# Score matmuls of a sparse-attention layer, all on 128 rows

## The reference, cut to what matters

```
s_c = jnp.einsum('bghqd,bgnd->bghqn', qblk, k_c) * scale + head_bias(rel_c)
...
s_s = jnp.einsum('bghqd,bgqkd->bghqk', qblk, k_sel) * scale + bias_s
...
s_w = jnp.einsum('bghqd,bgkd->bghqk', qblk, k_wb) * scale + head_bias(rel_w)
...
return gblk[..., 0:1] * o_c + gblk[..., 1:2] * o_s + gblk[..., 2:3] * o_w
```

## Time and profile before

| | |
|---|---|
| median of 3 runs | 2231.28 us (2228.06 to 2240.76) |
| the profiled execution | 2240.75 us, its span 2239.3 us |
| mean granted TensorE clock | 0.975 of full |
| TensorE busy | 2163.0 us, 97% |
| VectorE, ScalarE, GpSimd busy | 1216.4, 1016.4, 23.4 us |
| sparse attention, first score block to last product | 1903.31 to 2045.04 us |

### The profile page before, as it was taken

The page is one execution under the profiler, slowest core; times in us unless marked ns, Lnnn a source line. Parts: engine busy times, 40 slices in busy tenths (PEclk is TensorE's granted clock), DMA queues, the critical chain, the costliest instruction groups (busy, mean ns, idle before and its releaser), DMA issues.

```text
span 2239.3 us, 25951 instructions
## 1 busy us (share of the span) xinstructions
PE 2163.0 (97%) x10523; PEld 1779.0 (79%) x10523; DVE 1216.4 (54%) x1391; ACT 1016.4 (45%) x1334; POOL 23.4 (1%) x48
## 2 busy tenths in 40 slices
PE   8998999999999999999999999899999999998999
PEld 6887987888888776788888889788767887777887
DVE  5455677445545654644554457554544555655444
ACT  6444435344534554534453443443444445644342
POOL 1000000000000000000000000000000000000000
PEclk9999999999999999999999999999998999769999
DMA  7553425655655431565555535765438563113653
GB/s 258 187 178 123 151 96 195 199 169 188 210 187 175 132 127 57 183 200 181 188 180 196 169 132 179 210 202 192 123 122 188 169 204 119 38 38 113 199 177 113
DMA packets 265378, 361.01 MB, mean 161 GB/s; under 512 B 19855, under 2 KB 206651, under 8 KB 265132
## 3 DMA queue, kind: packets, MB, share of 16 engines
q1 hardware_dynamic: 256800, 351.57, 47.9%
q10 hardware_dynamic: 7772, 7.17, 1.9%
q0 software_dynamic: 688, 0.62, 0.1%
HBM read 357.75 MB, written 1.57 MB: 160 GB/s over the span
## 4 chain that ended last, share of the span: by engine, by line
PE 90%; DVE 5%; ACT 2%; issue 1%; ACTq 0%; DMA 0%; POOL 0%; SPq 0%; DVEq 0%
PE bank L388 18%; PE bank L390 17%; PE bank L389 17%; PE acc L649 6%; PE acc L650 6%; PE acc L648 6%; PE bank L383 2%; PE bank L384 2%; PE bank L385 2%; PE tr L629 2%; PE acc L1772 1%; PE acc L679 1%; PE acc L681 1%; PE tr L471 1%; PE acc L680 1%; DVE x_tok L777 1%
## 5 line engine op out<-in xcount | busy, mean ns | idle before, releaser
L388 PE MATMUL bank<-w_hi_,xt_hi_ 128*128 128x512 f32 x1760 | 712.0, 405 | 12.2 <-DVE h_tok L755 5.2
L412 DVE TENSOR_TENSOR w_lo_<-raw_in,w_hi_ 128x2048 fp32r<-128x2048 f32 (+1 forms) x321 | 571.9, 1789 | 240.8 <-ACT w_hi_ L402 240.7
L390 PE MATMUL bank<-w_hi_,xt_lo_ 128*128 128x512 f32 x1760 | 692.7, 394 | 0.0
L389 PE MATMUL bank<-w_lo_,xt_hi_ 128*128 128x512 f32 x1760 | 691.4, 393 | 0.0
L402 ACT ACTIVATE w_hi_<-raw_in 128x2048 fp32r<-128x2048 f32 (+1 forms) x321 | 479.3, 1507 | 84.2 <-PE bank L390 22.8
L760 DVE TENSOR_TENSOR wo_lo_<-raw_out,wo_hi_ 128x2048 fp32r<-128x2048 f32 x80 | 183.4, 2292 | 473.7 <-ACT wo_hi_ L725 473.7
L388 PEld LDWEIGHTS bank<-w_hi_,xt_hi_ 128*128 128x128 f32 x1760 | 334.0, 190 | 83.3 <-issue 6.9
L390 PEld LDWEIGHTS bank<-w_hi_,xt_lo_ 128*128 128x128 f32 x1760 | 333.6, 190 | 72.2
L389 PEld LDWEIGHTS bank<-w_lo_,xt_hi_ 128*128 128x128 f32 x1760 | 334.7, 190 | 62.8
L725 ACT ACTIVATE wo_hi_<-raw_out 128x2048 fp32r<-128x2048 f32 x80 | 153.3, 1916 | 359.5 <-PE acc L650 359.5
L648 PE MATMUL acc<-wo_hi_,ht_hi_ 128*128 128x512 f32 x576 | 224.1, 389 | 0.0
(11 more groups left out here) (308 smaller groups left out, 1882.4 us busy)
## 6 DMA issues: line engine op xcount, KB each, us to landing
raw_in<-ffn_w_in SPq DMA_DIRECT2D x352, 512.0 KB, 4.9
raw_out<-ffn_w_out SPq DMA_DIRECT2D x88, 1024.0 KB, 5.0
raw_in<-hg_w_in SPq DMA_DIRECT2D x16, 1024.0 KB, 5.2
raw_in<-fox_w_in SPq DMA_DIRECT2D x16, 1024.0 KB, 5.3
raw_in<-conv_w_in SPq DMA_DIRECT2D x12, 1024.0 KB, 5.1
raw_in<-hg_w_out SPq DMA_DIRECT2D x4, 1024.0 KB, 5.0
raw_in<-fox_w_out SPq DMA_DIRECT2D x4, 1024.0 KB, 5.1
raw_in<-conv_w_out SPq DMA_DIRECT2D x4, 1024.0 KB, 5.2
```

The source lines that it names most:

```text
L388: mm(o, g.xt_hi_[:, k, tok], wh[:, par, k, 0:w], start=first, stop=False)
L389: mm(o, g.xt_hi_[:, k, tok], wl[:, par, k, 0:w], start=False, stop=False)
L390: last = mm(o, g.xt_lo_[:, k, tok], wh[:, par, k, 0:w], start=False, stop=end)
L412: dve.e.tensor_tensor(g.piece(g.wl, n, half, k), raw, g.piece(g.wh, n, half, k).bitcast(F32), ALU.subtract).then_inc(g.w_lo, 4 if k is Non ...
```

## The change

All score matmuls work on 128 rows. The low parts of the keys stand on partitions 0 to 63 only, with zeros on 64 to 127, so that a full query tile times them gives the product of the query's high part alone. For this the high part of every query is on partitions 0 to 63: odd heads are stacked like even ones. ScalarE writes the zeros of the compressed keys, GpSimd those of the others (a tile minus itself), with a new semaphore, `ns_kzero`.

```
-            ins = pe.e.matmul(o, q[high], ns_keys(g.ol)[high, :, gr, 0:n], start=False, stop=True)
+            ins = pe.e.matmul(o, q, ns_keys(g.ol)[:, :, gr, 0:n], start=False, stop=True)
...
-                    ins = pe.e.matmul(o, q[high], g.kct2[high, gr, 1], start=False, stop=True)
+                    ins = pe.e.matmul(o, q, g.kct2[:, gr, 1], start=False, stop=True)
```

In the waits of `scores` there is one more, `pe.wait_ge(g.ns_kzero, gr + 1)`, and 3 becomes 4 for `kv_kct` there and in `pe_ffn`. The elementwise engines:

```
+        act.e.activation(g.kct2[DH:P, :, 1, 0:n], g.ident[DH:P, 0:GROUPS * n].rearrange("p (g n) -> p g n", g=GROUPS),
+                         ACT.Copy, scale=0.0).then_inc(g.kv_kct, 1)
...
-        dve.wait_ge(g.kv_kct, 2)
+        dve.wait_ge(g.kv_kct, 3)
         dve.e.scalar_tensor_tensor(
-            g.kct2[:, :, 1, 0:n], g.tr[0][:, 0:GROUPS * NB_CMP].rearrange("p (g n) -> p g n", g=GROUPS)[:, :, 0:n],
+            g.kct2[0:DH, :, 1, 0:n], g.tr[0][0:DH, 0:GROUPS * NB_CMP].rearrange("p (g n) -> p g n", g=GROUPS)[:, :, 0:n],
...
-            act.e.activation(ns_queries(g, h + odd)[high], g.tr[1][high, 0:T], ACT.Copy,
-                             scale=g.gains[high, G_NSAQ:G_NSAQ + 1]).then_inc(g.ns_qh, 1)
+            act.e.activation(ns_queries(g, h + odd)[0:DH], g.tr[1][high, 0:T], ACT.Copy,
+                             scale=g.gains[0:DH, G_NSAQ:G_NSAQ + 1]).then_inc(g.ns_qh, 1)
...
-        dve.e.tensor_tensor(ns_keys(g.ol)[:, :, gr], g.kt[:, :, gr], ns_keys(g.oh)[:, :, gr].bitcast(F32),
+        dve.e.tensor_tensor(ns_keys(g.ol)[0:DH, :, gr], g.kt[0:DH, :, gr], ns_keys(g.oh)[0:DH, :, gr].bitcast(F32),
...
-            dve.e.scalar_tensor_tensor(q[low], g.tr[1][high, 0:T], g.gains[high, G_NSAQ:G_NSAQ + 1],
-                                       q[high].bitcast(F32), ALU.mult, ALU.subtract).then_inc(g.ns_ql, 1)
+            dve.e.scalar_tensor_tensor(q[DH:P], g.tr[1][DH * odd:DH * odd + DH, 0:T], g.gains[0:DH, G_NSAQ:G_NSAQ + 1],
+                                       q[0:DH].bitcast(F32), ALU.mult, ALU.subtract).then_inc(g.ns_ql, 1)
...
 def pool_nsa(g, pool):
+
+    pool.wait_ge(g.narrow_mm, 2)
+    pool.wait_ge(g.kv_cb, NT)
+    for gr in range(GROUPS):
+        pool.wait_ge(g.ns_kzero, gr)
+        pool.e.tensor_tensor(ns_keys(g.ol)[DH:P, :, gr], g.kt[DH:P, :, gr], g.kt[DH:P, :, gr],
+                             ALU.subtract).then_inc(g.ns_kzero, 1)
+    pool.wait_ge(g.ns_kzero, GROUPS)
```

More of the change, by code:

```diff
@@ L94 @@
 kv_kc kv_rows8 kv_spread kv_vcb kv_kc_turned kv_kct
-ns_khi ns_klo
+ns_khi ns_klo ns_kzero
 ns_gain ns_gt ns_gt_turned ns_gates ns_stack ns_qh ns_ql ns_sc ns_s ns_m ns_exp ns_csc ns_turned ns_pt ns_pv ns_ob ns_o
@@ L621, in turn @@
         elif c == 0 and f == 6:
-            pe.wait_ge(g.kv_kct, 3)
+            pe.wait_ge(g.kv_kct, 4)
         for t in range(NT):
@@ L1640, in dve_compress_slot @@
     elif j == 16:
-        dve.wait_ge(g.kv_kct, 2)
+        dve.wait_ge(g.kv_kct, 3)
         dve.e.scalar_tensor_tensor(
-            g.kct2[:, :, 1, 0:n], g.tr[0][:, 0:GROUPS * NB_CMP].rearrange("p (g n) -> p g n", g=GROUPS)[:, :, 0:n],
-            g.gains[:, G_KN:G_KN + 1], g.kct2[:, :, 0, 0:n].bitcast(F32), ALU.mult, ALU.subtract).then_inc(g.kv_kct, 1)
+            g.kct2[0:DH, :, 1, 0:n], g.tr[0][0:DH, 0:GROUPS * NB_CMP].rearrange("p (g n) -> p g n", g=GROUPS)[:, :, 0:n],
+            g.gains[0:DH, G_KN:G_KN + 1], g.kct2[0:DH, :, 0, 0:n].bitcast(F32), ALU.mult, ALU.subtract).then_inc(g.kv_kct, 1)
 NS_TIMES = NSA_HEADS + 5
@@ L1726, in scores @@
     def scores(h):
-        gr, high = h * GROUPS // H, slice(DH * (h % 2), DH * (h % 2) + DH)
+        gr = h * GROUPS // H
         pe.wait_ge(g.ns_ql, h + 1)
@@ L1731, in scores @@
             pe.wait_ge(g.ns_gt, 1)
-            pe.wait_ge(g.kv_kct, 3)
+            pe.wait_ge(g.kv_kct, 4)
         pe.wait_ge(g.ns_klo, gr + 1)
+        pe.wait_ge(g.ns_kzero, gr + 1)
         for t in range(NT):
@@ L1954, in stack @@
         for odd in range(2):
-            q, high, low = ns_queries(g, h + odd), slice(DH * odd, DH * odd + DH), slice(DH - DH * odd, P - DH * odd)
+            q = ns_queries(g, h + odd)
             dve.wait_ge(g.ns_qh, h + odd + 1)
-            dve.e.scalar_tensor_tensor(q[low], g.tr[1][high, 0:T], g.gains[high, G_NSAQ:G_NSAQ + 1],
-                                       q[high].bitcast(F32), ALU.mult, ALU.subtract).then_inc(g.ns_ql, 1)
+            dve.e.scalar_tensor_tensor(q[DH:P], g.tr[1][DH * odd:DH * odd + DH, 0:T], g.gains[0:DH, G_NSAQ:G_NSAQ + 1],
+                                       q[0:DH].bitcast(F32), ALU.mult, ALU.subtract).then_inc(g.ns_ql, 1)
     def scores(h):
```

## The result

| | before | changed |
|---|---|---|
| median, first comparison | 2239.58 us (2228.06 to 2240.95, 5 runs) | 2219.24 us (2214.88 to 2222.23, 5 runs) |
| ratio, 95% interval | | 0.9927 (0.9907 to 0.9946) |
| median, measured again | 2232.78 us (2225.49 to 2241.11, 20 runs) | 2223.56 us (2215.44 to 2225.62, 10 runs) |
| ratio, 95% interval | | 0.9953 (0.9935 to 0.9970) |
| sparse attention, gates' turn to last product | 145.7 us | 130.0 us in both profiles |

The forecast was 2213.5 us against 2231.28, a ratio of 0.9920; the change made the kernel faster by 0.5 to 0.7%. The ratio is taken over all executions, so it is not that of the two medians (in the first comparison the means give 0.9923, the medians 0.9909). Medians and ratios leave out executions in the chip's slower state, of which there was one (3550.64 us, in e18).

What follows compares the result with a forecast made beforehand. TensorE, busy 97% of the span, was taken to bound the kernel and pace the heads. Full-clock blocks 9.5 plus half-clock 9.4 minus 1.0 gave 17.9 us off 2231.28: 2213.4, put down as 2213.5 us, range 2197 to 2222.

Steps and rivals of the forecast that it cites:

- The price of a block: Eight score matmuls of one head: 1.13 us at full clock, saving 1.06; 2.12 at half clock, saving 1.57.
- VectorE must keep up ... it moves as a whole. I subtract nothing: Sparse heads: VectorE, 8.45 us of work per two heads shrinking to 9.28, keeps pace; nothing subtracted.
- The 0.5 us a head that was left to the range: Nine full-clock heads: possible loss to VectorE, up to 4.5 us in all, allowed in the range only.
- VectorE takes part of it: Rival, sparse heads: 0.5 us a head lost to VectorE, 2218 us; chance 0.17 together with less gain by small matmuls.
- Hidden behind the key splits and the first query stack: GpSimd's first zeros, 3.4 us each, done by about 1900.7, before the first score block, with 2.6 us in hand.
- it was GpSimd's time that grew: Answer to whether zeros slow VectorE: in one row, a 128-element addition beside VectorE, GpSimd took 0.84 us.
- Six half-clock blocks at 1.57: The six of sixteen score blocks run at half clock save 1.57 us each, 9.4 us.
- the clock comes back: Rival: denser blocks lift the granted clock in the half-clock stretches, up to 14.3 us more, 2199 us; chance 0.22.
- its floor of 33 us: Clock rival, second half-clock stretch: without the dip, VectorE's 29.9 us and its waits bound it at about 33 us.
- The 1.0 us taken off for ScalarE's L1896: Block at 1958.17, before TensorE's 2.3 us wait for ScalarE: 1.0 us of its saving counted as lost.
- The wait for L1984: TensorE's wait for VectorE after the block at 1938.14, 2.4 us, would grow by a microsecond; that block saves 0.
- slower: Rival: longer waits drop the clock in the nine full-clock heads, 24 us slower, 2255 us; chance 0.04.

Runs made afterwards that it cites:

- e18: Changed kernel with zeros written earlier, VectorE's weight splits one head later, and an extra overwritten 512-column pair in heads 6 to 12; 2220.60 us, ratio 0.9949.
- e1: Changed kernel with all four low matmuls of a block back on 64 rows, new stacking and zeros kept; 2231.33 us, ratio 0.9979.
- e2: Changed kernel with GpSimd's zeros for key groups 3 and 2 written earlier, after the preceding feed-forward block; 2224.68 us, ratio 0.9939.
- e3: Changed kernel with two extra overwritten pairs of 512-column matmuls in every block, long but dense; 2221.30 us, ratio 0.9930.
- e15: Kernel before with two extra overwritten 512-column pairs on 128 rows in the blocks of heads 6 to 12 only; 2240.54 us, ratio 1.0007.
- e17: e12 with one extra overwritten pair of 512-column matmuls in the blocks of heads 6 to 12; 2214.93 us, ratio 0.9907.
- e12: Changed kernel with VectorE's splits of the second query chunk's weights each moved behind one more head's scores; 2214.34 us, ratio 0.9922.

## Why the sum came near and which steps failed, point by point

- **The price of a block** was right: 1.15 us for 1.13, small matmuls 0.11 apart for 0.107; at half clock 2.28 for 2.12, so 1.41 saved and not 1.57. The term taken from the nearest row (64 columns) held for 16 columns. The rule of the Trainium skill that load time goes by columns alone, "TensorE: Matmul & The Clock Gate", section "LDWEIGHTS (loading the stationary operand)", agrees with the loads themselves (0.18 us on 64 rows, 0.19 on 128). That the change would then be worth nothing does not follow: e1, which differs from the changed kernel in the row heights alone, has a stage of 145.6 us for 130.0. Load time is not the distance between starts, for with alternating heights the load shown did not run beside the matmul ahead. The rule of the Trainium skill that a change of tiling mode drains the engine, "TensorEngine Tiling (Array Packing)", section "Key Properties", leads the right way: a step costs 0.10 to 0.20 us here. That it is this drain no run shows.
- **"VectorE must keep up ... it moves as a whole. I subtract nothing": this step failed.** It followed one chain, from a block to the next query low parts, and that was not the binding one: the ring through ScalarE's exponentials and the two halves of the weight split takes 5.2 us a head, and two heads cannot be done in 9.28. From block 3 to 5 they took 10.5. The 0.5 us a head that was left to the range was 0.5 in head 3, 0.7 in head 4 and 1.2 in head 5, and head 2, with the norm in it, lost 1.9 (6.7 us from block 2 to 3, against 5.9 - 1.06). Block 6 to 7 took 8.5 us instead of 7.8. So where nothing was subtracted, 4.9 us went. The rival "VectorE takes part of it" was right about the place.
- **"Hidden behind the key splits and the first query stack": failed.** The zeros' own price was overstated (1.3 us each for 3.4), and they were done before block 0, as said. But "it was GpSimd's time that grew" was generalised from one row; here VectorE's splits went from 2.50 to 4.18 us, and block 0 came 1.7 us late. e2 shows it.
- **Six half-clock blocks at 1.57: mis-sized, and incomplete.** Blocks 7 to 11 saved 5 x 1.41 = 7.0 by themselves; the stretch gained 10.4, for the clock rose from 0.50 to 0.72. That is the rival "the clock comes back", in part; its floor of 33 us was too low, the stretch stops at 38 to 39. The 1.0 us taken off for ScalarE's L1896 (now L1899) came near: the wait for it grew from 2.3 to 3.5.
- **Last heads:** blocks 13 to 15 lie 9.2 us apart, 9.3 forecast. The clock was low again from 1979.1 to 1982.6 (0.51), into head 12, which starts at 1980.9; hence 2.5 and not 3.2.
- **The wait for L1984** grew by 0.9 us (1 forecast), and "slower" did not come: over the whole stage every kernel with its blocks on 128 rows was granted more, from 0.82 (e2) to 0.94 (e3) for 0.78, though from block 12 to 15 the changed kernel had 0.94 for 1.00.

The sum was near (15.7 for 17.9) because 6.5 us lost at block 0 and in heads 2 to 6 were met by 4.8 won where the clock had been low. The medians show 9.2 and 20.3 us in the two comparisons, with the clock elsewhere in between.

## What to carry to other kernels

Matmuls of different row heights in turns cost 0.1 to 0.2 us at each step at full clock; zeros below a half-height operand take that away at no cost in columns. When the pacing engine gets faster, walk the chain of the engines behind it through one whole turn, with every foreign instruction in their queues, and compare its length with the new pace: a busy share of 74% said nothing of a ring at 92% of the old pace (5.2 of 5.7 us). And an instruction given to an idle engine is not free if it runs beside another engine's: here GpSimd's zeros made VectorE's splits 1.7 us longer.

## What the runs showed of the hardware

- Two-input elementwise work on 64x512 elements took VectorE 678 ns alone and 1101 ns beside GpSimd's; GpSimd's own took 1.3 us each beside VectorE's and 1.1 (2.15 us for two) away from them.
- The granted clock rose when matmuls that compute nothing were added: 0.50 to 0.64 from block 7 to 12 (e15), where 20 more matmuls took 0.2 us; and 0.67 to 0.90 (e17 against e12).
- A step from 128 to 64 rows or back costs 16-column matmuls 0.10 us at full clock (0.11 to 0.21 between starts) and at half clock 0.10 as well (0.21 to 0.31).
